# Eight experts of a 256-token trunk: 128-slot split products against 96-slot plain fp32 products on 64- and 32-column tiles

## The reference, cut to what matters

```python
D_MODEL, SEQ, D_FF, N_EXPERTS, TOP_K = 1024, 256, 2816, 8, 2

def moe_swiglu(xn, w_router, w1, w3, w2):      # w1, w3: (8, 1024, 2816); w2: (8, 2816, 1024)
    xf = xn.reshape(-1, D)
    logits = (xf @ w_router).astype(jnp.float32)
    vals, idx = lax.top_k(logits, TOP_K)
    gates = jax.nn.softmax(vals, axis=-1)
    combine = jnp.sum(jax.nn.one_hot(idx, N_EXPERTS) * gates[..., None], axis=1)
    y = jnp.zeros_like(xf)
    for e in range(N_EXPERTS):
        y = y + combine[:, e:e+1] * swiglu(xf, w1[e], w3[e], w2[e])   # (silu(x@w1) * (x@w3)) @ w2
    return y
...
    h = h + moe_swiglu(rmsnorm(h, o_norm2), ...)
return rmsnorm(h, final_norm)
```

## Time and profile before

| | |
|---|---|
| median of three runs | 1199.6 us |
| the profiled execution | 1201.01 us, span 1199.3 us |
| experts, first product to last scatter | about 518.8 to 1189 us of the span |
| PE busy | 1148.1 us, 96% |
| DVE, ACT busy | 669.4 us (56%), 561.9 us (47%) |
| weights read from HBM in all | 348.89 MB, 292 GB/s over the span |

### The profile page before, as it was taken

How to read it: one execution, slowest core, us unless ns; L and a number is a source line. 1 busy time by engine, 2 the same in 40 slices (tenths; PEclk the granted TensorE clock), 3 DMA queues, 4 the chain that set the end, 5 groups by cost and what they waited for, 6 DMA issues and landing times.

```text
span 1199.3 us, 16296 instructions
## 1 busy us (share of the span) xinstructions
PE 1148.1 (96%) x6555; PEld 851.9 (71%) x6555; DVE 669.4 (56%) x744; ACT 561.9 (47%) x642; POOL 49.5 (4%) x93
## 2 busy tenths in 40 slices
PE   5989899999999999899999999999999999999986
PEld 5979778888879976685486788648668468487351
DVE  4875664554456523492384698328578058574054
ACT  4772355443444466452364577137356056264041
POOL 8010000000000022000000000000000000000000
PEclk9999999999999999989999999999999999999999
DMA  9632059755425822179999999999999999999992
GB/s 319 181 122 73 20 171 369 241 184 176 140 66 162 332 94 73 66 279 353 414 413 411 412 415 413 346 414 414 411 414 415 415 412 412 413 413 416 413 409 96
DMA packets 117025, 351.08 MB, mean 293 GB/s; under 512 B 8168, under 2 KB 55312, under 8 KB 116944
## 3 DMA queue, kind: packets, MB, share of 16 engines
q1 hardware_dynamic: 115840, 347.11, 75.6%
q0 software_dynamic: 1104, 2.86, 0.8%
HBM read 348.89 MB, written 1.05 MB: 292 GB/s over the span
## 4 chain that ended last, share of the span: by engine, by line
PE 89%; DVE 4%; DMA 2%; ACT 2%; POOL 2%; issue 1%; POOLq 0%; DVEq 0%; ACTq 0%; SPq 0%
PE ps L625 20%; PE ps L626 20%; PE ps L627 20%; PE ps L1737 11%; PE ps L1758 7%; PE ps L1681 3%; DMA room<-in_o_moe_w_dram 2%; PE ps L1693 1%; PE ps L1390 1%; POOL level L747 1%; PE ps L1598 1%; PE ps L1610 1%; DMA gam<-in_e_sgu_w_dram 1%; PE ps L1718 1%; PE ps L1715 1%
## 5 line engine op out<-in xcount | busy, mean ns | idle before, releaser
L1924 DVE TENSOR_TENSOR low<-room,all_hi 128x1408 fp32r<-128x1408 f32 (+1 forms) x216 | 307.8, 1458 | 197.8 <-ACT all_hi L889 197.3
L889 ACT ACTIVATE all_hi<-room 128x1408 fp32r<-128x1408 f32 (+1 forms) x216 | 264.9, 1255 | 255.5 <-DMA room<-in_o_moe_w_dram 174.9
L1737 PE MATMUL ps<-room,xg_raw 128*64 128x512 f32 (+1 forms) x768 | 152.5, 558 | 0.0
L625 PE MATMUL ps<-all_hi,xg_hi 128*128 128x512 f32 (+1 forms) x384 | 145.0, 378 | 1.4 <-DVE y_small L2378 1.0
L626 PE MATMUL ps<-low,xg_hi 128*128 128x512 f32 (+1 forms) x384 | 144.7, 377 | 0.0
L627 PE MATMUL ps<-all_hi,xg_lo 128*128 128x512 f32 (+1 forms) x384 | 144.2, 375 | 0.0
L625 PE MATMUL ps<-all_hi,x_hi 128*128 128x512 f32 (+1 forms) x336 | 125.2, 373 | 5.1 <-ACT xn L978 2.4
L626 PE MATMUL ps<-dense_lo,x_hi 128*128 128x512 f32 (+1 forms) x336 | 122.9, 366 | 0.0
L627 PE MATMUL ps<-all_hi,x_lo 128*128 128x512 f32 (+1 forms) x336 | 122.6, 365 | 0.0
L1737 PEld LDWEIGHTS ps<-room,xg_raw 128*64 128x64 f32 x768 | 54.6, 137 | 95.5 <-issue 95.3
L1917 DVE TENSOR_TENSOR dense_lo<-slots_a,all_hi 128x2048 fp32r<-128x2048 f32 x40 | 91.4, 2290 | 47.4 <-ACT all_hi L882 47.4
(11 more groups left out here) (370 smaller groups left out, 1572.2 us busy)
## 6 DMA issues: line engine op xcount, KB each, us to landing
room<-in_o_moe_w_dram SPq DMA_DIRECT2D x256, 704.0 KB, 15.4
room<-in_o_moe_w_dram SPq DMA_DIRECT2D x80, 1024.0 KB, 18.5
slots_c<-in_e_ffn_w_dram SPq DMA_DIRECT2D x36, 512.0 KB, 6.9
slots_a<-in_e_ffn_w_dram SPq DMA_DIRECT2D x30, 512.0 KB, 5.2
slots_a<-in_e_w_in_dram SPq DMA_DIRECT2D x24, 512.0 KB, 8.8
slots_a<-in_o_w_qkv_dram SPq DMA_DIRECT2D x18, 512.0 KB, 4.4
room<-in_o_moe_w_dram SPq DMA_DIRECT2D x16, 512.0 KB, 17.0
slots_a<-in_e_w_out_dram SPq DMA_DIRECT2D x8, 512.0 KB, 4.0
```

Of the source, the lines that this page charges most:

```text
L625: pe.matmul(o, a_hi, b_hi, start=first, stop=False)
L889: act.activation(unit_hi(st), raw_of(v, off, st.size), ACT.Copy).then_inc(hi_done, 1)
L1737: last = mm(ps[a * SMALL:(a + 1) * SMALL, o + b, 0:n], xg_raw[:, c, :], raw[a][:, c0:c0 + n], start=(c == 0), stop=(c == DC - 1))
L1924: tt(unit_lo(st), raw_of(v, off, st.size), unit_hi(st).bitcast(F32), ALU.subtract).then_inc(lo_done, 1)
```

## The change

Big experts get 96 slots instead of 128 and are no longer split: slots 0 to 63 are computed on two 64-column tiles (`up_first`, `down_first`), slots 64 to 95 on four 32-column tiles (`up_late`, `down_late`), all in plain fp32 from the weights as they landed. Steps are taken in pairs (`UNITS`): both steps' products of one tile size, then both of the other; the next pair begins with the size that the last one ended with. Expert 0's two halves come first, so that the order of the other experts is needed behind 39 transfers instead of 16; the ranking on DVE moves behind the first gather. The ring is 147 KB (37632 floats): it takes in the dense layers' `dense_hi` and `dense_lo` and 2816 floats behind the slots. The last small expert gets PSUM bank 3, and a few steps of scattering move. The overflow loop lists also tokens over 96 and over 224 of a big expert.

```diff
-    PHASE = [(0, 0), (1, 0), (0, 1)] + [(q, a) for q in range(2, NE) for a in range(2 if big(q) else 1)]
+    PHASE = [(q, a) for q in range(NE) for a in range(2 if big(q) else 1)]
+    QUART, WIDE, NARROW = HALF // 2, 384, 320
+    MANY_COLS = ((0, QUART // 2), (QUART // 2, QUART // 2), (QUART, WIDE))
+    LATE_COLS = ((0, WIDE), (WIDE, NARROW), (QUART, WIDE), (QUART + WIDE, NARROW))
+    UNITS = []
+    for st in STEPS:
+        if UNITS and big(st.q) and (UNITS[-1][-1].kind, UNITS[-1][-1].n) == (st.kind, st.n) and st.j % 2:
+            UNITS[-1].append(st)
+        else:
+            UNITS.append([st])
-    BEFORE, ROOM = SPLITS * DC * CW, (SPLITS + RING) * DC * CW
+    BEFORE, AFTER = 2 * SPLITS * DC * CW, 2 * HALF
+    ROOM = BEFORE + RING * DC * CW + AFTER
...
-            return 0 if q == 1 else 6                      # y_bank
+            return 3 if q == NE - 1 else 6
-        SCAT_AT = {q: ((7, (0, 1)), (9, (2, 3))) if big(q) else ((12, (0, 1)), (14, (2, 3))) for q in range(1, NE - 1)}
+        SCAT_AT = {q: ((7, (0, 1)), (9, (2, 3))) if big(q) else ((13, (0, 1)), (15, (2, 3))) for q in range(NE - 1)}
-        BACK_AT = {q: 5 if big(q) else 10 for q in range(1, NE - 1)}
+        BACK_AT = {q: 5 if big(q) else 11 for q in range(NE - 1)}
...
-            def split_step_hi(st):                         # ACT; DVE's split_step_lo goes too
-                act.activation(unit_hi(st), raw_of(v, off, st.size), ACT.Copy).then_inc(hi_done, 1)
...
+                    elif b == 0:                           # turn_up of a big expert
+                        for i in range(4):
+                            last = pe.transpose(o[:, i * P:(i + 1) * P], u_act[:, i * P:(i + 1) * P], ident[:, :])
+                    elif b == 1:
+                        pe.transpose(o[:, 0:P], u_act[:, 4 * P:5 * P], ident[:, :])
+                        for k in range(2):
+                            half = slice(k * SMALL, (k + 1) * SMALL)
+                            last = mm(o[half, P:P + SMALL], u_act[:, 5 * P:QUART], ident[:, half], start=True, stop=True)
+                    else:
+                        for i in range(3):
+                            pe.transpose(o[:, i * P:(i + 1) * P], u_act[:, QUART + i * P:QUART + (i + 1) * P], ident[:, :])
+                        last = mm(o[SMALL:P, at:at + LATE], u_act[:, QUART + 2 * P:QUART + NARROW], ident[:, 3 * LATE:P], ...)
...
+            def carry_back(q, t):                          # scatter of a big expert
+                for turn, cols, first in ((back, slice(0, 512), True), (back_r, slice(512, D), False)):
+                    for y in (y_hi, y_lo):
+                        for hf in range(2):
+                            rows = slice(hf * SMALL, (hf + 1) * SMALL)
+                            last = mm(ps[:, SCAT[q][2 * t + hf], :], turn[rows, t, :], y[rows, cols], ...)
...
+            def up_first(st):
+                for b, (c0, n) in enumerate(MANY_COLS[0:2]):
+                    for a in range(2):
+                        last = mm(ps[a * SMALL:(a + 1) * SMALL, o + b, 0:n], xg_many[:, c, 0:SMALL],
+                                  raw_of(v, a * QUART + c0, n), start=(c == 0), stop=(c == DC - 1))
+            def up_late(st):
+                for a, (c0, n) in enumerate(LATE_COLS):
+                    last = mm(ps[a * LATE:(a + 1) * LATE, o + 2, 0:n], xg_many[:, c, SMALL:MANY], raw_of(v, c0, n),
+                              start=(c == 0), stop=(c == DC - 1))
+            def down_first(st):                            # two matmuls of 512 columns
+                return sides(st, m_first(st.n)[:, st.part, :])
+            def down_late(st):
+                for k in range(4):
+                    at = k % 2 * CW
+                    last = mm(ps[k * LATE:(k + 1) * LATE, 7, at:at + CW], m_late(st.n)[:, j, :], raw_of(v, off + k * CW, CW), ...)
...
+            for unit in UNITS:
+                first, late = (up_first, up_late) if up else (down_first, down_late)
+                one, other = (late, first) if late_first else (first, late)
+                for st in unit:
+                    before_up(st) if up else before_down(st)
+                    arrived(st)
+                    one(st)
+                for st in unit:
+                    other(st).then_inc(raw_used, 1)
+                late_first = not late_first
```

More of the change, by code:

```diff
@@ L16 @@
 EPS = 1e-6
-Step = namedtuple("Step", "kind n q a j part size big at ends pieces")
-Piece = namedtuple("Piece", "kind q a part size big last")
+Step = namedtuple("Step", "kind n q a j part ends pieces")
+Piece = namedtuple("Piece", "kind q a part size group last")
 EXP_LN = "natural_log_exp_and_others"
@@ L131, in trunk @@
                 part, halves = (j // 2, j % 2), (a,) if big(q) else (0, 1)
-                on = [(new_piece(kind, q, half, part, HALF, big(q)), 0) for half in halves]
-                todo.append(Step(kind, n, q, a, j, part, HALF, big(q), 0, False, on))
+                if j % 2 == 0 or not big(q):
+                    GROUPS.append([])
+                todo.append(Step(kind, n, q, a, j, part, False, [(new_piece(kind, q, half, part, HALF), 0) for half in halves]))
         else:
@@ L178, in place_pieces @@
                 at = 0
-            mark = Mark("used", A_MOE + pc.last + 1) if pc.big else Mark("raw", pc.last + 1)
-            old = claim(taken, at, at + pc.size, mark)
+            old = claim(taken, at, at + pc.size, Mark("raw", pc.last + 1))
             where.append((at, *(max([m.n for m in old if m.kind == kind], default=0) for kind in ("lo", "used", "raw"))))
@@ L189, in arrive_sem, with transfers @@
     def arrive_sem(v):
-        return ARRIVE_ON[v % ARRIVE]
+        return ARRIVE_ON[PIECES[v].group % ARRIVE]
+    def transfers(v):
+        pc = PIECES[v]
+        return 2 if big(pc.q) and pc.kind == "down" and pc.part[1] == 1 else 1
     def arrive_base(k):
@@ L207, in trunk @@
         else:
[L208 to L241, removed]
+            free = max(PIECES[u].last for u in GROUPS[pc.group - ARRIVE]) + 1
+            if seen[2] < free:
+                late_waits.append((v, seen[2], free))
+                WHERE[v] = (*WHERE[v][0:3], free)
+                seen[2] = free
     w_in_cols = [QKV0 + CW * i for i in range(6)] + [GATE0, GATE0 + CW] + [SGU_W, SGU_W + CW] + [0, CW]
@@ L695, in load_piece @@
                     dst = raw_of(v, 0, pc.size)
+                elif big(pc.q):
+                    j, nb = pc.part
+                    both = o_moe_w2[0][bass.ds(e, 1), rows, :].rearrange("e (s r) d -> (e s) r d", s=2)
+                    r0 = j // 2 * P
+                    dst = raw_of(v, 0, pc.size)
+                    if nb == 2:
+                        src = both[:, r0:r0 + P, :].rearrange("s p d -> p s d")
+                        dst = dst.rearrange("p (s d) -> p s d", s=2)
+                    else:
+                        for s in range(2):
+                            sp.dma_start(dst[s * SMALL:(s + 1) * SMALL, :], both[s, r0:r0 + SMALL, :])\
+                                .then_inc(ring_in[arrive_sem(v)], 16)
+                        return
                 else:
@@ L1700, in way_back @@
                     last = pe.transpose(ps[0:SLOTS, bank, t * P:(t + 1) * P], sel_w[:, t, :], ident[:, :])
+                if big(q):
+                    for t in range(TILES):
+                        last = pe.transpose(ps[0:SLOTS, bank, SEQ + t * P:SEQ + (t + 1) * P], sel_r[:, t, :], ident[:, :])
                 last.then_inc(back_done, 1)
+            def carry_back(q, t):
[3 more added lines that the diff above has]
+                            rows = slice(hf * SMALL, (hf + 1) * SMALL)
+                            last = mm(ps[:, SCAT[q][2 * t + hf], :], turn[rows, t, :], y[rows, cols], start=first and y is y_hi,
+                                      stop=not first and y is y_lo)
+                            if not first and y is y_lo:
+                                last.then_inc(scat_done, 1)
             def scatter(q, parts=range(4)):
@@ L1712, in scatter @@
                     t, hf = m // 2, m % 2
-                    if big(q):
-                        for y, first in ((y_hi, True), (y_lo, False)):
-                            last = mm(ps[:, SCAT[q][m], :], turn[:, t, :], y[:, hf * 512:(hf + 1) * 512], start=first, stop=not first)
-                    else:
-                        rows = slice(hf * SMALL, (hf + 1) * SMALL)
-                        last = mm(ps[:, SCAT[q][m], :], turn[rows, t, :].bitcast(F32), y_small[rows, :], start=True, stop=True)
```

425 lines of the change are left out of this document (204 added, 221 removed).

## The result

The changed kernel takes 1208.9 us in the median of four runs (1205.4 to 1209.1), the kernel before 1199.8 us in the same comparison: a ratio of 1.0063, 95% interval 1.0045 to 1.0081. It is slower by 0.6%, where no change was forecast. The profiled execution is the quickest of the four, 1205.4 us with a span of 1203.6 us.

A forecast was written before the change was run, and what follows sets the result against it. PE was taken to set the pace, DMA just keeping up. Steps -20.3, switches +17.9, detours +10.2, silu +0.6 and removed waits -8.7 gave -0.3 on 1201.0, so 1200.7, predicted as 1199 us median, no change; range 1176 to 1226.

The forecast's parts named there:

- the part on transfers: Expert weights: 258.1 MB left at 518 us end near 1143 us; DMA would bind only if PE gained some 30 us.
- Wrong in kind: PE waiting for transfers in the middle of the experts: Sign named for a prediction wrong in kind: PE waits for transfers mid-experts; no chance of its own.
- the cover: Transfers running ahead of a faster PE: 26 pieces (18.7 MB) by 518 us; DMA binds only beyond some 30 us gained.
- the early start: Expert 0's second half first, 10 more pieces in the ring: some 17 us of transfers ahead, counted at nothing beyond 1.2 us.
- DMA shows idle time in the big phases: Sign named for a right prediction: DMA idles in big phases, since the ring is full.
- Steps: Big experts on PE: up steps 1.833 us instead of 1.927, down steps 1.293 instead of 1.387; 20.3 us less in all.
- the two rivals on them: Late products: four narrow tiles run dear (1215 to 1227 us, 0.13), or only two run at once (1306; 0.09 including overflow).
- Switches: Big phases: 112 changes between 64- and 32-column tiles at 0.16 us each, 17.9 us more.
- The rival of the free switch: Switching between 64 and 32 columns is free or nearly: 1181 us, or 1190 at half the price; chance 0.28.
- The wait for the bank: Last small expert no longer waits for the big one's sums to leave its bank: 2.3 us saved.
- Its sequel, 1.6 us of slower clock: Behind the bank wait, the last small expert's first five steps ran with clock at 0.93 of full: 1.6 us saved.
- the detours: Tile-size changes for turns, gathers and scatter in phases formerly all 128 columns wide, plus two transposes: 10.2 us more together.

The follow-up runs named there:

- the kernel of one transfer: Changed kernel, but each big half's last w2 piece is one transfer of 128 contiguous rows (neighbouring rows replace half): 1193.2 us, 0.9941 to the kernel before.

## Why the prediction was wrong

**The step that failed** is the part on transfers: "DMA would bind only if PE gained some 30 us". It had two things wrong.

It took the 413 GB/s of before for the time after. But the change cuts eight pieces into transfers of 64 rows, which stood in `load_piece` and in the count of `transfers`, and the working gave this edit no cost at all, not even a bound. The eight dips cost some 25 us of transfer time, an estimate: 20 us x (413 - rate) / 413, over eight windows of 332 to 374 and two neighbours of 381 and 390. (The first, 540 to 560 us, moves only 378 GB/s without the dip; counted from there it is 23.) 767 to 934 us alone is 15 GB/s short. "Wrong in kind: PE waiting for transfers in the middle of the experts" was named as what would show it, but no rival had it.

And the cover was not 30 us. The working let 413 GB/s run on from 518 us, so that the weights would end near 1143 us. Without dips they end near 1166 us, since 520 to 600 us move 324 GB/s: the ring is full, and SP waits for PE. That is some 17 of the 23 us, and takes back most of what the early start had won: in the kernel of one transfer started late they end only some 4 us later. "DMA shows idle time in the big phases" holds only there; in 767 to 934 us the share is 1.02 even in the kernel of one transfer. So of the 25 us of dips about half was covered, 10 to 11 us of it by the early start, and the rest reached PE: 12.6 us between the two last scatters.

The Trainium skill (SBUF — State Buffer, Door 1: The DMA port swizzle) states the rule: partitions 0 to 63 reach only half of the ports by which DMA writes, and 0 to 127 all. Under "Can I just issue two DMAs to hit both halves?" it adds that two transfers, one to each half, do not make up for it. The runs agree: dips with two halves, none with the even and the odd partitions. By the table of ports in the same section of the Trainium skill, the even partitions reach all ports, and so do the odd ones. By the Trainium skill's 27.2 GB/s a port, 512 KB through half of them would take 2.4 us instead of 1.2, an estimate of 1.2 us a dip; measured are some 3. So the rule fits which transfers cost, and not how much; the runs show the partitions, and that the ports are the reason is the rule's account. It spoke against this change, and the prediction did not weigh it.

On the size the trace adds one thing: in a dip everything is slower, not only the 64 rows. Packets of 5632 bytes belong to the pieces of w1 and w3, which are 128 partitions wide. From 802 to 810 us they take 322 to 359 ns (medians of the four 2-us windows), and 219 ns in the window behind it.

**Steps.** Right: 1.18 + 0.645 = 1.825 us for a big up step (forecast 1.833); four narrow tiles run at full rate, and the two rivals on them fall. A late step is 384 columns x 1.684 ns = 0.647 us at the rate of the 64-column tiles, and 0.645 is measured. The 2.38 times for three narrow tiles of the Trainium skill (TensorE: Matmul & The Clock Gate, Part 3) doesn't show here; the measurement decides.

**Switches.** Right in kind; the price is 0.144 instead of 0.16, so 16.1 us instead of 17.9. The rival of the free switch falls. That a change of the tiling mode drains the engine (the Trainium skill, TensorEngine Tiling (Array Packing), Key Properties) agrees with it.

**Stalls.** The wait for the bank is right: 2.3 us, as forecast. Its sequel, 1.6 us of slower clock, is not in the trace of the run that brings the wait back; the times say 3.7 us for both (forecast 3.9), with 1.6 to 5.9 left open.

**Detours and the sum.** Without the dips the span is 1190.5 us, 8.8 less than before (7 by the ratio of the times), where the forecast was 0.3 less. The first product starts 1.2 us earlier (517.60 in the timeline of the kernel of one transfer, 518.79 before). From it to the last small up phase it is 581.2 us instead of 582.5; from there to the last scatter 81.3 instead of 86.8; behind that 0.8 less. In the first stretch steps (128 x (1.825 - 1.927) - 77 x 0.094 = -20.3), 106 switches (+15.3), the waits of before that lie there (-2.1: 1.1 for selection matrices, 1.0 for the second expert's sums), three small up phases of 37.79 instead of 37.94 (-0.5) and the silu (+0.6) make -7.0, and it got 1.3 shorter, so the detours cost some 5.7 us there, where about 9.7 were counted. No run took the detours apart; this is what is left over.

So the 1199 us stands 9.9 us under the result by two errors of opposite sign. By the medians the kernel without dips takes 1193.2 us: PE gained 5.8 us more than the forecast, and the transfers cost 15.7 (14.6 by the ratios) that weren't counted. That the range (1176 to 1226) held the result is luck: its upper end stood for dear narrow tiles, which did not come.

## What to carry to other kernels

Where PE and DMA both run full, cost every transfer whose shape the change touches, not only the bytes: look which partitions each one fills, and give 128 of them, or spread 64 over all, rather than one half. A full DMA share says nothing of the rate; read GB/s beside it, in windows short enough to show one piece. When a faster engine brings no time, undo the smallest edit of the other limit first: here it was worth some 15 us. And take the time at which the transfers end from a ring that fills, not from bytes over rate.

## What the runs showed of the hardware that was not expected

Two transfers of 64 rows, each to 64 neighbouring partitions, slow all that moves beside them (one alone was not run): 237 to 291 GB/s for some 8 us, at a full share, for 512 KB that would take 1.3 us at 413. The same rows to every other partition cost nothing (415 GB/s). To cut one product in two (288 and 64 columns) cost only 0.01 us, and four 32-column fp32 tiles stream as fast as two of 64 (0.645 us for a widest part of 384 columns, 1.68 ns a column).
